# Release points of bulk loads and casts in a hybrid attention and SSM block on eight cores

## The chip, the cores and the metric

The kernel runs on the 8 cores of one Trainium2 chip. Every core takes one of the 8 sequences and the whole set of weights, and the cores don't speak to each other. The metric is the device time of the slowest core. Each core has a matrix engine (TensorE: PE for its matmuls, PEld for its weight loads), a vector engine (VectorE, DVE), a scalar engine (ScalarE, ACT), GpSimd (POOL) and a queue engine (SyncE, SP). Transfers are issued on two queues: SP's, which carries plain copies and transposes, and POOL's, which carries the bulk weight loads that cast float32 to bf16 on the way.

## The reference, cut to what matters

One decoder block over 2048 tokens of width 2048. One input projection gives q, k, v and the SSM's input u; attention over a window of 128 and an S5 state-space model (SSM) run side by side; their normed outputs go through one output projection and a SwiGLU.

```
proj = rms_norm(x) @ w_in                     # 2560 columns: q 1024, k 256, v 256, u 1024
attn = sliding_window_attention(rotary(q), rotary(k), v, sinks)
z    = gelu(s5_ssm(u))                        # 64 groups of 16 channels, 64 complex states each
ssm  = z * sigmoid(z @ w_glu + b_glu)
h    = x + rms_norm(concat[rms_norm(attn), rms_norm(ssm)] @ w_o)
out  = h + rms_norm((silu(n @ w_gate) * (n @ w_up)) @ w_down),  n = rms_norm(h)
```

## The kernel before, in words

**How the order comes about.** The program is first recorded as a list of operations with their dependencies. A planner (`Prog.schedule`) then walks through it with cost formulas for each engine and both DMA queues, and always gives an engine the ready operation with the smallest `prio`. What comes out is one fixed order for each engine. On the chip every engine works through its order strictly; an operation that waits holds up all behind it on the same engine. All recorded operations carry the line of the planner's emit loop (L433), so that they are told apart by their tiles.

**The stages.** x is normed and transposed into `xnT`. `proj_u(0)` and `proj_u(1)` make u in 32 steps of 16 matmuls each (`usteps[0]` to `usteps[31]` are the ScalarE copies that end them); their weights lie in `ws[0]` and `ws[1]` (ws.6 and ws.7 in the profile). The SSM works on 32 pairs of groups (`ssm_pair(q)`), in eight batches of four pairs. Each batch b needs tables from `prep(b)`: `A1s[b % 2]` (A1.44, A1.45) is computed on VectorE and transposed by DMA into `A1Ts[b % 3]` (A1T.67 to A1T.69); `Kst` is copied by eight small DMAs into `KTs[b % 3]` (KT.73 to KT.75). `prep(b)` for b of 3 to 7 stands behind pairs 3, 7, 11, 15 and 19. A new `A1s` tile may be written only when the transpose that reads its old content has landed. The pairs have the smaller `prio` (10 to 41), the projections the larger one, so that the steps of `proj_u(1)` (100), v (200), k (210) and q (220 and more) fill the matrix engine where the SSM leaves it free.

**The loads around the change.** `load_h` loads one piece of 256 columns of `w_in` (1 MB in bf16) into one of the three buffers `wh` (wh.8 to wh.10): v, k, and then q in four pieces. wh.8 and wh.9 lie over `ws[0]`, wh.10 over the second half of `ws[1]`. The loads of v and k wait for the SSM's second u tile (`ur`, 1). A piece of q consists of two stretches of 128 columns that lie 256 columns apart, and is loaded by two DMAs. `cast_wo` casts one of 16 rows of `w_o` into a scratch tensor: nine wait for steps of u, seven for pairs of the SSM; four casts of `w_glu` (`glscr`) also wait for pairs. Their readers come much later, with the GLU and the output projection.

**The end of the output projection.** `oproj(tt)` normalizes a tile of 128 tokens, and a DMA transpose brings `hn` (hn.145, one buffer) into `hnT`. Then `gate_up(0)` starts: `unit(0, u)` loads a raw piece of `w_gate` or `w_up` of 1 MB (`raw`), VectorE makes five combinations of it (`wsm`), and 7 products of 8 matmuls follow, two of them straight from `raw`. Unit 2 of the first block has a buffer of its own, `raw2` (raw.153), over the sixth output weight tile, and its load waits for the transpose of tile 14. The accumulators of unit 2 begin with the two `ev` buffers that lie over `hn`.

Of the kernel before, what the change touches and what calls it, by code (L numbers as in the profile page):

```python
# [481 lines left out]
def build_nc():  # L482
    nc = bass.Bass("TRN2", target_bir_lowering=False, dynamic_dma_scratch_size=8192)

    def din(name, shape, dt=F32):
        return nc.dram_tensor(name, list(shape), dt, kind="ExternalInput").ap()
# [10 lines left out]
    w_in = din("w_in", [D, 2560])  # L497
# [15 lines left out]
    def sb(nm, off, shape, dt):  # L513
        cnt[0] += 1
        return nc.alloc_sbuf_tensor_at("%s.%d" % (nm, cnt[0]), list(shape), dt, offset=BASE + off)
# [4 lines left out]
    P = Prog(nc)  # L520
    V, A, G, T = P.V, P.A, P.G, P.T
    with ExitStack() as st:
# [53 lines left out]
        w_in_v = w_in.rearrange("(c p) n -> p c n", p=128)  # L576
# [203 lines left out]
        usteps = []  # L780
# [25 lines left out]
        qr2 = [sb("qr2", RK + 6144 + 1024 * i, [128, 512], BF16) for i in range(2)]  # L806
        nh_ = [0]

        def load_h(segs, rk=()):
            w = wh[(0, 1, 2, 0, 1, 2)[nh_[0]]]  # L810
            nh_[0] += 1
            o_ = 0
            for c0, n in segs:
                P.dma(w[:, :, o_:o_ + n], w_in_v[:, :, c0:c0 + n], q="gpsimd", rk=rk)
                o_ += n
            return w

# [228 lines left out]
        hn = sb("hn", CO, [128, 2048], BF16)  # L1046
# [7 lines left out]
        def cast_wo(n, op):  # L1054
            P.dma(woscr[n // 2, :, n % 2, :], w_o_v[:, n, :], q="gpsimd", after=(op,), wk=[("wo", n // 2, n % 2)])
# [59 lines left out]
        def next_ev(blk, lo=0):  # L1115
            n = len(ev[blk]) - lo
            ne[0] += 1
            return ev[blk][lo + ne[0] % n][:, :]
# [27 lines left out]
        def product(lhs, rhs):  # L1146
            bk = pbk[0] % 8
            pbk[0] += 1
            with P.group():
                for c in range(8):  # L1150
                    T.matmul(ps[:, bk, :], lhsT=lhs(c), rhs=rhs[:, c, :], start=(c == 0), stop=(c == 7))
            return ps[:, bk, :]

        def unit(blk, u, w_v, s):
            par = (u + blk) % 2
            r, m = raw[blk][par], wsm[blk][par]
            if blk == 0 and u == 2:
                r = raw2
            P.dma(r[:, :, :], w_v[:, :, s * 256:(s + 1) * 256], q="gpsimd", wk=[("gu", blk, u)],
                  rk=[("hn", 14)] if blk == 0 and u == 2 else (), lat=12.0 if blk == 0 and u < 2 else 0.0)  # L1160
            a11, a21 = r[:, 0:8, 0:128], r[:, 0:8, 128:256]
            a12, a22 = r[:, 8:16, 0:128], r[:, 8:16, 128:256]
            V.tensor_tensor(out=m[:, 0, :, :], in0=a11, in1=a22, op=ALU.add)
            V.tensor_tensor(out=m[:, 1, :, :], in0=a21, in1=a11, op=ALU.subtract)
            V.tensor_tensor(out=m[:, 2, :, :], in0=a21, in1=a22, op=ALU.add)
            V.tensor_tensor(out=m[:, 3, :, :], in0=a11, in1=a12, op=ALU.add)
            V.tensor_tensor(out=m[:, 4, :, :], in0=a12, in1=a22, op=ALU.subtract)
            n1, n2, n3 = xe[blk]
            (b11, b12), (b21, b22) = XB
            acc = {k: [next_ev(blk), False] for k in (21, 12, 11, 22)}  # L1170

            def into(k, prod, sign):
                o_, seen = acc[k]
                if seen:
                    V.tensor_tensor(out=o_, in0=o_, in1=prod, op=ALU.add if sign > 0 else ALU.subtract)
                else:
                    A.activation(out=o_, in_=prod, func=AF.Copy, scale=float(sign))
                    acc[k][1] = True
            how = {1: (lambda c: m[:, 0, c, :], n3, ((11, 1), (22, 1))),
                   2: (lambda c: m[:, 2, c, :], b11, ((21, 1), (22, -1))),  # L1180
                   3: (lambda c: r[:, c, 0:128], b12, ((12, 1), (22, 1))),
                   4: (lambda c: r[:, 8 + c, 128:256], n1, ((21, 1), (11, 1))),
                   5: (lambda c: m[:, 3, c, :], b22, ((12, 1), (11, -1))),
                   6: (lambda c: m[:, 1, c, :], n2, ((22, 1),)),
                   7: (lambda c: m[:, 4, c, :], b21, ((11, 1),))}
            for i in (4, 2, 5, 7, 6, 3, 1) if blk == 0 and u == 0 else (4, 3, 1, 2, 5, 6, 7):
                lhs, rhs, uses = how[i]
                prod = product(lhs, rhs)
                for k, sign in uses:
                    into(k, prod, sign)  # L1190
            return [acc[k][0] for k in (21, 12, 22, 11)]
# [104 lines left out]
        for q in range(32):  # L1296
            P.prio = 10.0 + q
            ssm_pair(q)
            P.prio = 60.0 + q
            last = P.ops[-1]  # L1300
            if q in (8, 10, 12, 14, 16, 18, 20):
                cast_wo(9 + (8, 10, 12, 14, 16, 18, 20).index(q), last)
            if q in (9, 13, 17, 21):
                i = (9, 13, 17, 21).index(q)
                P.dma(glscr[:, i, :], w_glu_v[:, 4 + i, :], q="gpsimd", after=(last,), wk=[("gl", i)])
            if q % 4 == 3 and q < 20:
                P.prio = q - 4.0
                prep(q // 4 + 3)
# [2 lines left out]
        V.memset(v1[:, 1:17, :, 64:65], 1.0)  # L1311
        ur = [("ur", 1)]
        P.prio = 59.0
        wv = load_h(((1280, 256),), ur)
        wk_ = load_h(((1024, 256),), ur)
        P.prio = 200.0
        proj_h("v", wv)
        P.prio = 210.0
        proj_h("k", wk_)
        def load_q(a):  # L1320
            c0 = 512 * (a // 2) + 128 * (a % 2)
            return load_h(((c0, 128), (c0 + 256, 128)))
        P.prio = 59.0
        wq = [load_q(a) for a in (0, 1)]
        for a in range(2):
            P.prio = 220.0 + 10 * a
            proj_h("q", wq[a], 2 * a)
        P.prio = -300.0
        zconv()
        P.prio = 59.0  # L1330
        wq = [load_q(a) for a in (2, 3)]
        for tt in range(NT):
            P.prio = 240.0 + tt
# [45 lines left out]
def _host_layouts(inp):  # L1379
    f32 = np.float32  # L1380
    sm = np.zeros((128, NSM), f32)
    half = 32
    sm[:, C_INVF:C_INVF + 32] = (np.float32(10000.0) ** (-np.arange(half, dtype=f32) / np.float32(half))).astype(f32)[None, :]
    sm[:, C_SINK:C_SINK + 16] = inp["sinks"][0][None, :]
    sm[:, C_KT:C_KT + 17] = np.concatenate([np.arange(7, -1, -1), np.arange(0, 9)]).astype(f32)[None, :]
    sm[:, C_DSK:C_DSK + 64] = np.tile(inp["d_skip"][0].T, (8, 1))
    a_re, a_im, ldt = inp["a_re"][0], inp["a_im"][0], inp["log_dt"][0]
    b2 = np.zeros((128, 2, 32, 16), f32)
    c2 = np.zeros((128, 2, 32, 16), f32)
    for b in range(2):  # L1390
        rows = slice(64 * b, 64 * b + 64)
        sm[rows, C_ARA:C_ARA + 32] = a_re[b::2, :].T
        sm[rows, C_AIA:C_AIA + 32] = a_im[b::2, :].T
        sm[rows, C_LDA:C_LDA + 32] = np.broadcast_to(ldt[b::2][None, :], (64, 32))
        b2[rows, 0] = inp["b_re"][0][b::2].transpose(1, 0, 2)
        b2[rows, 1] = inp["b_im"][0][b::2].transpose(1, 0, 2)
        c2[rows, 0] = inp["c_re"][0][b::2].transpose(2, 0, 1)
        c2[rows, 1] = inp["c_im"][0][b::2].transpose(2, 0, 1)
    gv = np.zeros((5, D), f32)
    gv[0] = inp["g_pre_mix"][0]  # L1400
    gv[1] = inp["g_post_mix"][0]
    gv[2] = inp["g_pre_ffn"][0]
    gv[3] = inp["g_post_ffn"][0]
    gv[4, :1024] = inp["g_attn_out"][0]
    r = np.arange(1024)
    pm = (r // 128) * 128 + 16 * (r % 8) + (r % 128) // 8
    w_in = np.concatenate([inp["w_in"][0][:, :1536], inp["w_in"][0][:, 1536:][:, pm]], axis=1)
    w_glu = inp["w_glu"][0][pm][:, pm]
    w_o = np.concatenate([inp["w_o"][0][:1024], inp["w_o"][0][1024:][pm]], axis=0)
    sm[:, C_GSSM:C_GSSM + 8] = inp["g_ssm_out"][0][pm].reshape(8, 128).T  # L1410
    sm[:, C_BGLU:C_BGLU + 8] = inp["b_glu"][0][pm].reshape(8, 128).T
    return {
        "smalls": sm, "gvecs": gv, "ident": np.eye(128, dtype=f32),
        "ctab": np.broadcast_to(np.arange(256, dtype=f32)[None, :], (128, 256)).copy(),
        "b2": b2.reshape(128, 2, 512), "c2": c2.reshape(128, 2, 512),
        "w_in": np.ascontiguousarray(w_in), "w_glu": np.ascontiguousarray(w_glu),
        "w_o": np.ascontiguousarray(w_o), "w_gate": np.ascontiguousarray(inp["w_gate"][0]),
        "w_up": np.ascontiguousarray(inp["w_up"][0]), "w_down": np.ascontiguousarray(inp["w_down"][0]),
    }
# [14 lines left out]
```

How the kernel before makes its waits and increments, by code:

```python
            def run(eng, e):  # L420
                for op in self.order[e]:
                    w = waits[op.idx]
                    att = None
                    if w and e != "tensor":
                        att = w[0]
                        w = w[1:]
                    for s, v in w:
                        eng.wait_ge(sems[s], v)
                    if op.load is not None:
                        eng.preload_act_table_set(SET_NAME[op.load])
                    inst = None
                    for (m, a, kw) in op.calls:
                        inst = getattr(eng, m)(*a, **kw)
                        if att is not None:
                            inst._wait_ge(sems[att[0]], att[1])
                            att = None
                    if op.dma:
                        inst.then_inc(sems[op.sem], 16)
                    elif op.signal:
                        inst.then_inc(sems[e], 1)
                if e == "sync":
                    for d in self.last_dmas:
                        eng.wait_ge(sems[d.sem], d.val)
```

## Time and profile before

| | us |
|---|---|
| median of 3 runs (2609.4 to 2612.86) | 2612.28 |
| the profiled execution | 2606.16 |
| span of its slowest core (core 5) | 2604.6 |
| PE busy in the span | 2469.4 (95%) |
| DVE busy | 1556.5 (60%) |
| ACT busy | 827.4 (32%) |
| POOL busy | 567.3 (22%) |

A wait is listed with the engine that waits and the operation whose end released it. The granted clock is a share of TensorE's full speed. "To landing" is the time from a DMA's issue to the moment it is complete. The profiled execution's own time is 1.6 us above the span of its slowest core.

### The profile page before, as it was taken

The numbers are of one execution on the slowest core, as the hardware profiler recorded it, in microseconds if no ns is written. First come the engines' busy times: TensorE is split into PE (matmuls) and PEld (weight loads), VectorE is DVE, ScalarE is ACT, GpSimd is POOL, SyncE is SP. The second block draws the span as 40 slices with busy tenths as digits, with TensorE's granted clock in tenths as the row PEclk, the third lists the DMA queues.
The fourth block names the chain that finished last, engine by engine and source line by source line (L and its number), as shares of the span: only waits on it lengthen the run. The fifth ranks groups of instructions, "written<-read, shape, count | busy, mean of one in ns | idle before, by whom it ended". The sixth has DMA issues, their size and how long they took to land.

```text
span 2604.6 us, 33566 instructions; the slowest of 8 cores (2585.3 to 2604.6 us)
## 1 busy us (share of the span) xinstructions
PE 2469.4 (95%) x12896; PEld 1207.0 (46%) x12896; DVE 1556.5 (60%) x2436; ACT 827.4 (32%) x1634; POOL 567.3 (22%) x650
## 2 busy tenths in 40 slices
PE   4999889988999889999999999999999999999998
PEld 2545658843444334444444444444444444444443
DVE  6856674768767688777777300017888887710003
ACT  5534443376555432322222000003222223200002
POOL 0235735754333200100101111100100101111112
PEclk9878879999999999999999999999999999999999
DMA  9688837576778987676666967749999966775557
GB/s 241 167 132 122 116 92 97 86 185 164 195 172 194 195 147 123 83 95 82 88 91 86 189 105 110 109 69 158 181 176 177 139 88 83 95 120 76 75 105 241
DMA packets 463643, 341.80 MB, mean 131 GB/s; under 512 B 180224, under 2 KB 424320, under 8 KB 454528
## 3 DMA queue, kind: packets, MB, share of 16 engines
q0 software_dynamic: 260944, 173.10, 49.5%
q1 hardware_dynamic: 202544, 166.57, 25.6%
q8 instruction: 106, 1.74, 0.3%
q14 instruction: 49, 0.40, 0.1%
HBM read 406.65 MB, written 63.96 MB: 181 GB/s over the span
## 4 chain that ended last, share of the span: by engine, by line
PE 81%; DMA 7%; DVE 7%; ACT 2%; issue 2%; POOL 1%; SPq 0%; POOLq 0%; ACTq 0%; DVEq 0%
PE ps L433 81%; DMA ws.6_48<-w_in 2%; DVE M1.2_44 L433 1%; DMA KT.73_115<-Kst.54_96 1%; DVE ast.26_68 L433 1%; DVE ast.27_69 L433 1%; DMA raw.151_193<-w_up 1%; DMA PT.129_171<-Pb.125_167 1%; DMA A1T.67_109<-A1.45_87 1%; DMA PT.129_171<-Pb.126_168 1%; DVE xr.140_182 L433 1%; DMA hnT.146_188<-hn.145_187 0%; DVE hn.145_187 L433 0%; DMA zraw.111_153<-zscr 0%; DMA A1T.69_111<-A1.45_87 0%
## 5 line engine op out<-in xcount | busy, mean ns | idle before, releaser
L433 ACT ACTIVATE ps<-ps 128x512 f32<-128x512 f32 x96 | 55.8, 581 | 351.6 <-DVE ev.179_221 L433 138.5
L433 DVE TENSOR_TENSOR hf.238_280<-ps,gpo.193_235 128x512 f32<-128x512 f32 x16 | 11.1, 691 | 243.4 <-ACT junk.147_189 L433 233.6
L433 PE MATMUL ps<-hnT.146_188,wsm.154_196 128*128 128x512 bf16 x528 | 121.0, 379 | 1.1 <-DVE wsm.154_196 L433 1.1
L433 PE MATMUL ps<-hnT.146_188,wsm.155_197 128*128 128x512 bf16 x528 | 121.1, 379 | 0.0
L433 PE MATMUL ps<-hnT.146_188,wsm.157_199 128*128 128x512 bf16 x528 | 121.1, 379 | 0.0
L433 PE MATMUL ps<-hnT.146_188,wsm.156_198 128*128 128x512 bf16 x528 | 121.1, 379 | 0.0
L433 DVE TENSOR_TENSOR wsm.157_199<-raw.152_194 128x1024 bf16<-128x1024 bf16 x110 | 68.9, 684 | 85.3 <-DMA raw.152_194<-w_gate 83.2
L433 ACT ACTIVATE junk.147_189<-ps 128x512 bf16<-128x512 f32 x16 | 9.6, 597 | 253.4 <-PE ps L433 253.4
L433 POOL DMA_DIRECT2D raw.152_194<-w_gate x22 | 25.2, 1145 | 257.1 <-PE ps L433 160.1
L433 PEld LDWEIGHTS ps<-hnT.146_188,wsm.154_196 128*128 128x128 bf16 x528 | 51.6, 98 | 63.6 <-issue 1.6
L433 PEld LDWEIGHTS ps<-hnT.146_188,wsm.155_197 128*128 128x128 bf16 x528 | 51.7, 98 | 62.3
L433 PEld LDWEIGHTS ps<-hnT.146_188,wsm.157_199 128*128 128x128 bf16 x528 | 51.7, 98 | 62.3
L433 PEld LDWEIGHTS ps<-hnT.146_188,wsm.156_198 128*128 128x128 bf16 x528 | 51.7, 98 | 62.3
L433 POOL DMA_DIRECT2D raw.151_193<-w_up x22 | 25.1, 1140 | 252.5 <-PE ps L433 136.6
L433 DVE TENSOR_TENSOR wsm.156_198<-raw.151_193 128x1024 bf16<-128x1024 bf16 x110 | 70.1, 683 | 15.9 <-DMA raw.151_193<-w_up 15.9
L433 POOL DMA_DIRECT2D raw.150_192<-w_up x22 | 25.2, 1144 | 248.2 <-DVE wsm.154_196 L433 163.6
L433 PE MATMUL ps<-xnT.1_43,ws.7_49 128*128 128x512 bf16 x256 | 71.5, 446 | 0.0
L433 POOL DMA_DIRECT2D raw.149_191<-w_gate x21 | 24.1, 1149 | 214.1 <-PE ps L433 181.4
L433 DVE TENSOR_TENSOR wsm.154_196<-raw.149_191 128x1024 bf16<-128x1024 bf16 x105 | 65.5, 684 | 8.5 <-DMA raw.149_191<-w_gate 8.5
L433 DVE TENSOR_TENSOR wsm.155_197<-raw.150_192 128x1024 bf16<-128x1024 bf16 x110 | 68.6, 682 | 0.0
L433 PE MATMUL ps<-xnT.1_43,ws.6_48 128*128 128x512 bf16 x256 | 66.2, 424 | 1.1 <-DVE xnT.1_43 L433 1.0
L433 DVE TENSOR_TENSOR Ab.142_184<-ps,gpm.143_185 128x512 f32<-128x512 f32 x64 | 43.5, 686 | 39.0 <-PE ps L433 38.2
(1371 smaller groups left out, 6232.1 us busy)
## 6 DMA issues: line engine op xcount, KB each, us to landing
raw.150_192<-w_up POOLq DMA_DIRECT2D x22, 1024.0 KB, 9.4
raw.152_194<-w_gate POOLq DMA_DIRECT2D x22, 1024.0 KB, 13.2
raw.151_193<-w_up POOLq DMA_DIRECT2D x22, 1024.0 KB, 12.4
raw.149_191<-w_gate POOLq DMA_DIRECT2D x21, 1024.0 KB, 9.3
woscr<-w_o POOLq DMA_DIRECT2D x16, 512.0 KB, 11.6
xr.140_182<-x SPq DMA_DIRECT2D x8, 1024.0 KB, 6.3
xr.141_183<-x SPq DMA_DIRECT2D x8, 1024.0 KB, 7.1
hscr<-xr.140_182 SPq DMA_DIRECT2D x8, 1024.0 KB, 4.7
```

The source lines that it names most:

```text
L433: inst = getattr(eng, m)(*a, **kw)
```

## The change

- v's load now also waits for `usteps[22]`, k's for `usteps[27]` (both in `proj_u(1)`).
- The last three casts of `w_o` move from pairs 16, 18 and 20 to pairs 20, 22 and 24; the last two of `w_glu` from pairs 17 and 21 to 19 and 23.
- The host orders the columns of q so that a piece is one stretch of 256 columns. It is loaded by one DMA where there were two; the data in the buffer are the same.
- The load of `raw2` waits for the transpose of tile 15, the last one, in place of tile 14.

```diff
-        def load_h(segs, rk=()):
+        def load_h(segs, rk=(), after=()):
...
-                P.dma(w[:, :, o_:o_ + n], w_in_v[:, :, c0:c0 + n], q="gpsimd", rk=rk)
+                P.dma(w[:, :, o_:o_ + n], w_in_v[:, :, c0:c0 + n], q="gpsimd", rk=rk, after=after)
...
-                  rk=[("hn", 14)] if blk == 0 and u == 2 else (), lat=12.0 if blk == 0 and u < 2 else 0.0)
+                  rk=[("hn", 15)] if blk == 0 and u == 2 else (), lat=12.0 if blk == 0 and u < 2 else 0.0)
...
-            if q in (8, 10, 12, 14, 16, 18, 20):
-                cast_wo(9 + (8, 10, 12, 14, 16, 18, 20).index(q), last)
-            if q in (9, 13, 17, 21):
-                i = (9, 13, 17, 21).index(q)
+            if q in (8, 10, 12, 14, 20, 22, 24):
+                cast_wo(9 + (8, 10, 12, 14, 20, 22, 24).index(q), last)
+            if q in (9, 13, 19, 23):
+                i = (9, 13, 19, 23).index(q)
...
-        wv = load_h(((1280, 256),), ur)
-        wk_ = load_h(((1024, 256),), ur)
+        wv = load_h(((1280, 256),), ur, (usteps[22],))
+        wk_ = load_h(((1024, 256),), ur, (usteps[27],))
...
-            c0 = 512 * (a // 2) + 128 * (a % 2)
-            return load_h(((c0, 128), (c0 + 256, 128)))
+            return load_h(((256 * a, 256),))
...
+    qc = np.arange(1024).reshape(2, 2, 2, 128).transpose(0, 2, 1, 3).reshape(1024)
```

## Rows read from the trace of the kernel before

**Rows 1.** All cores: span and mean granted clock.
```profile
core 0: 2602.2 us, clock 0.970
...
core 5: 2604.6 us, clock 0.963
```
**Rows 2.** Core 5, chain that ended last: start, duration, what.
```profile
144.04 14.61 DMA A1T.67_109<-A1.45_87
...
302.59 20.91 DMA KT.73_115<-Kst.54_96
...
929.62 12.75 DMA hnT.146_188<-hn.145_187
```
**Rows 3.** Core 5, VectorE in order: start, duration, operation [idle before, releaser].
```profile
158.67 0.69 DVE L433 TENSOR_TENSOR A1.45_87<-TT.50_92,TT.51_93 128x512 bf16<-128x512 f32 x1 [12.17 <-DMA A1T.67_109<-A1.45_87]
...
188.78 1.35 DVE L433 TENSOR_TENSOR A1.44_86<-TT.50_92,TT.51_93 128x512 bf16<-128x512 f32 x1
```
**Rows 4.** Core 5, TensorE in order, SSM: columns as in the group before.
```profile
163.27 0.37 PE L433 MATMUL ps<-pab.100_142,identb.16_58 128*128 128x256 bf16 x1 [3.81 <-DVE Rb.104_146 L433]
...
167.08 6.36 PE L433 MATMUL ps<-xnT.1_43,ws.7_49 128*128 128x512 bf16 x16
...
325.18 0.37 PE L433 MATMUL ps<-uring.91_133,KT.75_117 128*128 128x256 bf16 x1 [2.10 <-ACT Kst.54_96 L433]
```
**Rows 5.** Core 5, slices: busy time by engine, then clock, DMA share, GB/s.
```profile
150.00:160.00 10.00, 9.46 (x40) 3.74 (x38) 1.33 (x3) 1.72 (x4) 1.65 (x3) 0.81 1.31 155
160.00:170.00 10.00, 6.49 (x21) 2.51 (x22) 9.56 (x20) 3.92 (x11) 1.79 (x2) 0.56 1.06 152
```
**Rows 6.** Core 0, TensorE in order.
```profile
160.93 0.37 PE L433 MATMUL ps<-pab.100_142,identb.16_58 128*128 128x256 bf16 x1 [12.41 <-DVE Rb.104_146 L433]
```
**Rows 7.** Core 5, POOL in order, bulk loads alone.
```profile
132.94 1.15 POOL L433 DMA_DIRECT2D wh.8_50<-w_in  x1 [2.49 <-DMA uring.90_132<-uscr]
...
135.19 1.16 POOL L433 DMA_DIRECT2D wh.9_51<-w_in  x1
...
204.84 1.16 POOL L433 DMA_DIRECT2D wh.10_52<-w_in  x1 [3.83 <-PE ps L433]
...
918.66 1.14 POOL L433 DMA_DIRECT2D raw.153_195<-w_gate  x1 [19.00 <-PE ps L433]
```
**Rows 8.** Core 5, SP's queue in order.
```profile
183.35 1.22 SPq L433 DMA_TRANSPOSE A1T.68_110<-A1.44_86  x1
```
**Rows 9.** Core 5, DMA issues of 150 to 200: KB each, us to landing.
```profile
A1T.68_110<-A1.44_86 SPq DMA_TRANSPOSE x1, 2.9
```
**Rows 10.** Core 5, DMA issues of 230 to 260.
```profile
wh.10_52<-w_in POOLq DMA_DIRECT2D x1, 512.0 KB, 8.8
```
**Rows 11.** Core 5, DMA issues of 385 to 400.
```profile
zraw.111_153<-zscr SPq DMA_DIRECT2D x1, 512.0 KB, 11.0
```
**Rows 12.** Core 5, PE waits of 0 to 1100: us in total, times, longest.
```profile
PE ps L433 <- DMA zraw.111_153<-zscr: 4.9, 1, 4.9
```
**Rows 13.** Core 5, DMA issues of 840 to 1000.
```profile
raw.149_191<-w_gate POOLq DMA_DIRECT2D x4, 1024.0 KB, 10.4
...
raw.153_195<-w_gate POOLq DMA_DIRECT2D x1, 1024.0 KB, 12.7
```
**Rows 14.** Core 5, TensorE in order, start of the gate and up products.
```profile
931.62 1.89 PE L433 MATMUL ps<-hnT.146_188,raw.153_195 128*128 128x512 bf16 x8 [3.46 <-DMA raw.153_195<-w_gate]
...
946.85 1.89 PE L433 MATMUL ps<-xe.159_201,wsm.154_196 128*128 128x512 bf16 x8 [1.25 <-DVE ev.179_221 L433]
949.85 5.34 PE L433 MATMUL ps<-hnT.146_188,wsm.154_196 128*128 128x512 bf16 x24 [1.11 <-DVE wsm.154_196 L433]
```
**Rows 15.** Core 5, VectorE there.
```profile
933.09 3.09 DVE L433 TENSOR_TENSOR wsm.155_197<-raw.150_192 128x1024 bf16<-128x1024 bf16 x5
```
**Rows 16.** Core 5, ScalarE there.
```profile
942.39 0.60 ACT L433 ACTIVATE ev.180_222<-ps 128x512 f32<-128x512 f32 x1 [6.69 <-DMA hnT.146_188<-hn.145_187]
```
**Rows 17.** Core 5, tile hnT from 840 to 975: landing of its five transposes.
```profile
DMA to landing us min/median/max: 3.8/5.2/12.8
```

More of the change, by code:

```diff
@@ L1406, in _host_layouts @@
     pm = (r // 128) * 128 + 16 * (r % 8) + (r % 128) // 8
-    w_in = np.concatenate([inp["w_in"][0][:, :1536], inp["w_in"][0][:, 1536:][:, pm]], axis=1)
+    qc = np.arange(1024).reshape(2, 2, 2, 128).transpose(0, 2, 1, 3).reshape(1024)
+    w_in = np.concatenate([inp["w_in"][0][:, :1024][:, qc], inp["w_in"][0][:, 1024:1536], inp["w_in"][0][:, 1536:][:, pm]], axis=1)
     w_glu = inp["w_glu"][0][pm][:, pm]
```

## The prediction

> **What bounds the kernel now.** I read the cores first: core 5 ends last, core 0 is 2.4 us behind it [rows 1]. A saving counts only as far as the core that ends last has it. Then the page: TensorE is busy for 95% of the span, and its idle time lies in the first 950 us, where the SSM and the output projection are; from there on the gate, up and down products run without a gap. So a change pays by the TensorE time that it frees ahead of 950, in idle time or in clock. The chain of waits shows where transfers stand on the path: a transpose of the SSM's tables of 14.61 us, small copies of 20.91 us, and the last transpose of the output projection of 12.75 us [rows 2].
>
> The first of them is the clearest stall. VectorE stands for 12.17 us at a write to A1.45 that needs the transpose issued at 144.04 [rows 3]. In flight are the loads of v and k, issued at 132.94 and 135.19 [rows 7]. A transpose of the same size with no bulk load beside it landed in 2.9 us [rows 8, 9]. VectorE's order holds the SSM's own steps behind that write. TensorE fills the time with two steps of u and then idles 3.81 us [rows 4]; its clock was 0.81 before and falls to a mean of 0.56, between the levels of 1.2 and 2.4 GHz, in the ten microseconds after [rows 5]. Core 0 idles 12.41 us at the same place [rows 6]: it ran the filler at a higher clock and was through with it sooner. The core that ends last is thus the one that this stall costs least.
>
> **The change part by part, on core 5.**
>
> *v's load.* It leaves 133. The step `usteps[22]` is the one that ends at 167.08 + 6.36 = 173.4 [rows 4]; with the ScalarE copy behind it I take 174.4 for the issue. The stall that goes is worth the idle 3.81 us and the slow clock: of 6.49 us busy at 0.56, at 0.81 only 6.49 x 0.56 / 0.81 = 4.49 would have been needed, 2.0 us [rows 4, 5]. Sum -5.8. That is the upper bound of the gain; the lower is nothing, if the casts still in flight hold the transpose long enough. I take all of it, since the two large loads are the bulk of what is in flight. No engine waits longer for v: u's steps run until about 230, and a load of 1 MB has a median of 10.4 us [rows 13].
>
> What is late next: the transpose of A1T.68 at 183.35 [rows 8]. It was alone and landed at 186.3, and VectorE wrote A1.44 without a wait at 188.78 [rows 3]. Now v's load is in flight, from 174.4 to about 185 alone, and to about 190 with the cast that is released by the same step. If the transpose lands at 191, VectorE stalls 2 us, and TensorE's filler of one step covers nearly all. At the worst it takes 14.61 us as A1T.67 did [rows 2], lands at 198, and the 9.2 us stall stands bare: 0 to +9.2, I take +1.
>
> The Trainium skill, page "DMA: Bandwidth & Descriptors", section "Queues, rings and completion order", has each DMA engine alternate between the queues that have work, a packet at a time. By that rule a transpose beside one loaded queue would take about twice its 2.9 us, an estimate of 5.8, and A1.44 would wait 0.4 us. The rows here don't bear that out: 14.61 against 2.9 is five times. I keep +1; by the rule it would be 0.
>
> *k's load and the first piece of q.* The first half of that piece was issued at 204.84, when TensorE had read the last of what lay there [rows 7]; that is the step after which k's load is now released. The piece itself, now one transfer, can start only where its second half did, after the last step of u. So at 205 1 MB takes the place of half a megabyte, 10.4 against 8.8 us [rows 10, 13], beside the transpose whose VectorE wait is the second stall of this stretch. -1 (a little less in flight, should k come later) to +4 (the whole load in its way); I take +1, near the difference of 1.6. Behind the waiting issue on POOL stand the same table steps as before, since POOL waited for the same step.
>
> *Casts.* The five moved casts are read after 500 us; their own delay costs nothing, as 100 us and more of projections lie between. Their issues (about 0.6 us each) go to POOL places where the pairs' own waits are already. What they and the halved second piece of q leave is the stretch around 300, where the copies of KT.73 took 20.91 us [rows 2], ScalarE's next Kst copy waited for them and TensorE for that, 2.10 us [rows 4]. I take -2.1 (bounds 0 and -2.1, plus what the clock adds). The cover at 310 to 345 is thin, but the KT copies issued then are first read some 20 us later.
>
> *q in one stretch.* Its effect is on the last z tile: TensorE waits 4.9 us [rows 12] for a load that took 11.0 us [rows 11] beside two half loads of q. Two halves at 8.8 us make 17.6 us of queue, one whole load 10.4 [rows 10, 13]; 7 us less lies beside the z tile. Bounds 0 and -4.9; I take half, -2.5.
>
> *raw2 held back.* Before, its load was issued at 918.66, and what released it was TensorE's last read of the output weights under it [rows 7], not tile 14. Tile 15's transpose is issued at 929.62 [rows 2]. What that transpose delays now is ScalarE: `ev.180` lies over `hn` and waits 6.69 us [rows 16], and VectorE with it. So unit 2 could not be evacuated early anyhow; but its products could run. TensorE's idle time from there to 955 was 3.46 + 1.25 + 1.11 = 5.8 us [rows 14]. Now: at 931.62 - 3.46 = 928.2 TensorE has nothing until the first combination of unit 1, 933.09 + 0.6 [rows 15], which is 5.5 us. Five products at 5.34 / 3 = 1.78 us [rows 14] from 933.7 end at 942.6. With raw.153 out of the way the transpose takes less than 12.75, but more than the median of 5.2 [rows 17], since the load of unit 4 is still in flight: I take 8, so 937.6. Load issue and landing, 0.3 + 10.4 [rows 13], make 948.3, so 5.7 us idle. Together 11.2 against 5.8: +5.4, and with the clock that falls behind gaps of this length +6. Bounds: with 3.8 us for the transpose the load lands at 944.1, +1.2; with 12.75 and a load of 12.7 [rows 13] it lands at 955.4, 12.8 us idle, +12.5. Unit 3's load can be no cover: it is issued behind or beside this one on the same queue.
>
> *Sum:* -5.8 + 1 + 1 - 2.1 - 2.5 + 6 = -2.4 us on a span of 2604.6. The execution's own time was 2606.16, which becomes 2603.8. The median of the runs is 6.1 us above that execution; the same difference makes 2609.9.
>
> On a core like core 0 the first term is -12.4 and more, so its sum is near -9; but core 5 sets the end. A difference below 0.2%, 5.2 us, can't be told from none here.
>
> **The rivals.**
>
> *The stall is worth its full size.* If in the timed runs a core like core 0 ends last, the first term is -12.41 - 2.0 [rows 5, 6], A1T.68 takes back 3, k's load 1, q gives -2.5, and with a transpose of tile 15 near its median the hold-back costs 1.2: -11.7; core 5 itself would be at -2.4 - 4.8 = -7.2. By a value between the two the time is about 2603. For it: core 0 is only 2.4 us behind [rows 1], and one execution doesn't fix which core ends last. Against: the profile has core 5 last, and by rows 5 its filler runs at 0.81.
>
> *The stall only moves.* v's load makes A1T.68 what A1T.67 was; the 5.8 us come back, +4.8 on my sum: 2614.7. For it: the release lies 9 us ahead of that transpose. Against: one load in place of two.
>
> *The hold-back decides.* Tile 15's transpose doesn't get faster, because the load of unit 4 alone is enough to hold it; raw.153 lands at 955, TensorE idles there once for 5.5 and once for 12.8 us, and runs at the lower clock after the long one as after 3.81 us in rows 5, for 2 us. +12.5 + 2 in place of +6 turns the sum of -2.4 into +6.1: 2618.4, slower. It decides from a landing of raw.153 later than about 954. For it: 12.7 and 12.75 are what the rows of before have. Against: a third of what was in flight is gone.
>
> *Nothing of it reaches the end.* The planner's order shifts with every changed release, and gains and losses of a few microseconds elsewhere cover it: 2612. I count it with the forecast.
>
> **How the numbers follow.** Forecast 0.37 (own range 2606 to 2615), full-sized stall 0.32, moved stall 0.09, hold-back 0.22. Faster: 0.32 and 0.04 of the forecast's lower edge, 0.36. Slower: 0.22 and 0.02 of its upper edge, 0.24. The rest, 0.40, is no change. The range goes from 2598, below the full-sized stall by what a still better tile 15 gives, to 2620, just over the hold-back case.
>
> **What would show each step.** The write to A1.45 without a wait, and A1T.67 landing in under 7 us, show the first term; VectorE's idle time before A1.44 shows whether it moved. PE's wait for `zraw` below 3 us shows q's. The KT copies around 300 below 12 us show the casts'. For the hold-back: the landing of the last `hnT` transpose, the landing of raw.153, and PE's longest idle time between 925 and 960. The prediction is wrong if core 5's idle time there stays below 7 us, if A1T.68 takes over 12 us, or if another core ends last with the whole of the first stall saved.

## The result and the profile after

Nine runs of the changed kernel have a median of 2631.47 us, nine of the kernel before on the same chip 2612.49. In some executions, whatever the kernel, the four cores of one die run some per cent longer at a lower granted clock; the ratios and mean spans of this document leave those out. The ratio is 1.0073, 95% interval 1.0053 to 1.0093: **slower by about 19 us**, where the forecast was 2609.9 and the range ended at 2620. The profiled execution took 2629.61 us. Cores 0 and 5, which stood at 2602.2 and 2604.6 [rows 1]:

```profile
core 0: 2628.0 us, clock 0.963
...
core 5: 2616.4 us, clock 0.965
```

The two stretches that the prediction spoke of are both worse. First the SSM. These are the queues that issue, on core 0, which now ends last (start, duration, operation): SP's, then POOL's bulk transfers.

```profile
138.75 15.12 SPq L433 DMA_TRANSPOSE A1T.67_109<-A1.45_87  x1
...
181.74 1.57 SPq L433 DMA_TRANSPOSE A1T.68_110<-A1.44_86  x1
```
```profile
130.25 0.57 POOL L433 DMA_DIRECT2D woscr<-w_o  x1
...
135.16 0.56 POOL L433 DMA_DIRECT2D woscr<-w_o  x1 [2.56 <-ACT ust.76_118 L433]
...
137.51 0.54 POOL L433 DMA_DIRECT2D woscr<-w_o  x1 [1.79 <-ACT ust.76_118 L433]
...
147.08 0.57 POOL L433 DMA_DIRECT2D woscr<-w_o  x1 [4.12 <-ACT ust.76_118 L433]
...
175.56 1.22 POOL L433 DMA_DIRECT2D wh.8_50<-w_in  x1
```

v's load is away from 133 and comes at 175.56, as the diff says. But the casts of the output weights, released by u's steps, are still there, and A1T.67 has not become faster. The DMA issues of 120 to 260 on core 0 (us to landing), before and after:

```profile
A1T.67_109<-A1.45_87 SPq DMA_TRANSPOSE x1, 18.0
A1T.68_110<-A1.44_86 SPq DMA_TRANSPOSE x1, 2.8
```
```profile
A1T.67_109<-A1.45_87 SPq DMA_TRANSPOSE x1, 20.1
A1T.68_110<-A1.44_86 SPq DMA_TRANSPOSE x1, 9.7
```

Over the eight cores A1T.67 takes 19.7 to 24.7 us, where it took 14.6 to 20.3, and A1T.68 on seven of them 9.0 to 11.0 (5.9 on core 5), where it took 2.8 or little more. The transpose is not alone in being late. `uring.91`, a load of u that SP issues just ahead of A1T.67, took 9.6 to 13.0 us before and takes 18.7 to 20.5 now. Core 0, before and after (DMA issues of 120 to 160):

```profile
uring.91_133<-uscr SPq DMA_DIRECT2D x1, 512.0 KB, 10.0
```
```profile
uring.91_133<-uscr SPq DMA_DIRECT2D x1, 512.0 KB, 19.8
```

VectorE and TensorE of core 0 there, in order (in brackets the idle time before and its releaser):

```profile
158.89 0.69 DVE L433 TENSOR_TENSOR A1.45_87<-TT.50_92,TT.51_93 128x512 bf16<-128x512 f32 x1 [19.56 <-DMA A1T.67_109<-A1.45_87]
...
191.49 1.26 DVE L433 TENSOR_TENSOR A1.44_86<-TT.50_92,TT.51_93 128x512 bf16<-128x512 f32 x1 [4.11 <-DMA A1T.68_110<-A1.44_86]
```
```profile
163.49 0.37 PE L433 MATMUL ps<-pab.100_142,identb.16_58 128*128 128x256 bf16 x1 [13.89 <-DVE Rb.104_146 L433]
...
193.49 0.37 PE L433 MATMUL ps<-pab.100_142,identb.16_58 128*128 128x256 bf16 x1 [4.34 <-DVE Rb.104_146 L433]
```

The 12.41 us of [rows 6] are 13.89, and a second stall has come behind it, at the write that had no wait in [rows 3]. Core 5, on which the prediction was worked out, lost more: its idle 3.81 [rows 4] became 14.27.

```profile
164.38 0.37 PE L433 MATMUL ps<-pab.100_142,identb.16_58 128*128 128x256 bf16 x1 [14.27 <-DVE Rb.104_146 L433]
```

The slices of [rows 5] show it (busy time by engine, then clock, DMA share, GB/s):

```profile
150.00:160.00 10.00, 0.10 (x1) 0.00 (x0) 0.22 (x1) 0.00 (x0) 0.00 (x0) 0.65 1.01 184
160.00:170.00 10.00, 5.38 (x19) 2.19 (x20) 9.56 (x20) 2.81 (x8) 1.79 (x2) 0.50 0.01 2
```

The second holds the finding in one row: the DMA share is 0.01, TensorE runs at the lower of its levels, 1.2 GHz, after a slice without work, and the transfers are through: what was lost here was lost waiting for them.

Then the output projection. TensorE of core 0, in order:

```profile
945.09 2.72 PE L433 MATMUL ps<-xe.160_202,wsm.155_197 128*128 128x512 bf16 x6 [5.76 <-DVE wsm.155_197 L433]
...
964.69 3.27 PE L433 MATMUL ps<-xe.158_200,raw.153_195 128*128 128x512 bf16 x8 [8.18 <-DMA raw.153_195<-w_gate]
```

and the chain that ended last on this core (start, duration, what), in which the transpose and the load now follow one another:

```profile
940.78 12.10 DMA hnT.146_188<-hn.145_187
...
953.61 10.95 DMA raw.153_195<-w_gate
```

All eight cores idle 5.76 us at `wsm.155` and 3.8 to 14.5 at raw.153, where they had one wait of up to 5.5 [rows 14]. TensorE's idle time of 900 to 990 is 10.8 to 21.5 us a core, 15.0 in the mean, and was 6.1.

From the last z matmul and the last of the output projection one reads where the 22 us lie by which the mean span of the profiled cores grew (2596.4 to 2618.1): the last z matmul comes 6.7 us later (408.4 to 415.1), the stretch between the two grew by 3.5, and the stretch from the output projection's end by 11.5 (1686.1 to 1697.6).

### The profile page after: what moved, and what is told of

It reads as the page before. It is cut to its first block, busy times and chain, and to the rows that moved or that the text cites. A ratio compares the mean times of both kernels' runs of the same rounds, so it can differ in the third digit from the quotient of the medians.

```text
span 2628.0 us, 33350 instructions; the slowest of 8 cores (2605.8 to 2628.0 us)
## 1 busy us (share of the span) xinstructions
PE 2446.8 (93%) x12687; PEld 1204.9 (46%) x12896; DVE 1547.8 (59%) x2436; ACT 826.9 (31%) x1634; POOL 568.3 (22%) x646
## 4 chain that ended last, share of the span: by engine, by line
PE 73%; DMA 12%; DVE 8%; issue 3%; ACT 3%; POOL 1%; POOLq 0%; SPq 0%; DVEq 0%
PE ps L433 73%; DMA raw.151_193<-w_up 2%; DMA raw.152_194<-w_gate 2%; DMA ws.6_48<-w_in 2%; DMA hf.238_280<-hscr 1%; DVE ast.26_68 L433 1%; DMA A1T.69_111<-A1.45_87 1%; DMA A1T.67_109<-A1.45_87 1%; DVE ast.27_69 L433 1%; DVE M1.2_44 L433 1%; DMA PT.129_171<-Pb.125_167 1%; DVE xr.140_182 L433 1%; DMA PT.129_171<-Pb.126_168 1%; DMA zraw.111_153<-zscr 0%; DMA hnT.146_188<-hn.145_187 0%
## 5 line engine op out<-in xcount | busy, mean ns | idle before, releaser
L433 DVE TENSOR_TENSOR wsm.156_198<-raw.151_193 128x1024 bf16<-128x1024 bf16 x110 | 70.2, 685 | 16.3 <-DMA raw.151_193<-w_up 16.3
L433 PE MATMUL ps<-wh.9_51,xnT.1_43 128*128 128x256 bf16 x512 | 65.9, 286 | 0.0
L433 PE MATMUL ps<-wh.10_52,xnT.1_43 128*128 128x256 bf16 x512 | 61.3, 277 | 0.0
## 6 DMA issues: line engine op xcount, KB each, us to landing
raw.152_194<-w_gate POOLq DMA_DIRECT2D x22, 1024.0 KB, 11.3
woscr<-w_o POOLq DMA_DIRECT2D x16, 512.0 KB, 10.2
```

Of the source, the lines that this page charges most:

```text
L433: inst = getattr(eng, m)(*a, **kw)
```

## The experiments

Each takes one part of the change, or answers one question. Their profiled spans scatter from core to core, and the slowest of eight decides a run; so beside each ratio (against runs of the kernel before on the same chip) I give a second figure: the mean span of each die's four cores, and of those means the median over all runs. It is 2598 us for the kernel before (2597.8 and 2598.3 in the two longest series) and 2617.2 for the change: +19, as by the ratio. I call it the mean span below, and its differences are taken from 2598. In the two shorter series of the kernel before, on the chips of e1 to e8, it is about 2600, so differences of 2 us are not told from none.

**The hold-back alone (e1, e9).** The kernel before with one word changed; measured twice. The ratio is the second's.

```
-                  rk=[("hn", 14)] if blk == 0 and u == 2 else (), ...
+                  rk=[("hn", 15)] if blk == 0 and u == 2 else (), ...
```

> The kernel before with one edit: raw2's load waits for tile 15's transpose. Theory A (the hold-back is the larger part of the loss): PE idles about 5.8 us at unit 1's combinations and 4 to 9 us at raw.153, where it idled 1 to 5.5 us, the clock falls behind both, and the time is 8 to 13 us above the kernel before (about 2622). Rival B (the loss comes from the SSM's releases, the hold-back is repaid because ScalarE no longer waits at ev.180): within 4 us of the kernel before.

> The kernel before with unit 2's load released by tile 15's transpose in place of tile 14's, and nothing else; its profile alone (an earlier run) has a last Wo product to end of span 10.7 us longer as a mean of the cores. Theory A (the hold-back costs what its idle time costs): 2612 + 10 = 2622, 2620 to 2625. Theory B (the SSM's loss makes the change's loss, the hold-back is nearly covered): within 0.2% of 2612.

Measured: ratio 1.0022 [0.9998, 1.0045]; mean span 2607.6, +9.5. In the profiles of both runs the stretch behind the output projection grew by 10.7 and 10.9 us, while the last z matmul came as before. Core 4 of the second run, TensorE:

```profile
939.19 3.57 PE L433 MATMUL ps<-xe.160_202,wsm.155_197 128*128 128x512 bf16 x8 [5.76 <-DVE wsm.155_197 L433]
958.19 3.54 PE L433 MATMUL ps<-xe.158_200,raw.153_195 128*128 128x512 bf16 x8 [7.60 <-DMA raw.153_195<-w_gate]
```

Idle time at 900 to 990 is 13.6 us a core (from 6.1), and the mean clock of 900 to 1000 fell from 0.98 to 0.94. The price is 9 to 11 us by mean span and trace; by the ratio alone, whose interval reaches from 0 to 11.7 us, it would not be settled.

**The change without the hold-back (e2).** The edit above taken back.

> The changed kernel with raw2's load released by tile 14 again; all else of the change stays. Theory A: 8 to 13 us below the changed kernel, so 5 to 10 us above the kernel before, the rest of the loss lying in the SSM (last z tile 4 to 10 us later than before in the mean of the cores). Rival B: it stays near the changed kernel, 15 us or more above the kernel before.

Measured: 1.0064 [1.0043, 1.0086]; mean span 2613.0, +15. The last z matmul is 8.7 us late. This is the second theory's number: taken out of the whole change, the hold-back gives back 2 us by the ratios and 4 by mean span, although the stretch behind the output projection is 9.0 us shorter than in the changed kernel. So the prices don't simply add, and at least half of the loss is the SSM's.

**The release of v and k alone (e3, e12).** Measured twice; the ratio is the second's.

```
-        wv = load_h(((1280, 256),), ur)
-        wk_ = load_h(((1024, 256),), ur)
+        wv = load_h(((1280, 256),), ur, (usteps[22],))
+        wk_ = load_h(((1024, 256),), ur, (usteps[27],))
```

> The kernel before with one edit: the loads of v and k released by steps 22 and 27 of u. Theory C (A1T.67 was not held up by these loads but by the casts of w_o and what else is in flight, and v's load now holds A1T.68): A1T.67 lands in 14 to 20 us as before, PE idles 12 us or more behind it, a new idle time of 4 to 5 us appears near 194, and the time is 3 to 8 us above the kernel before. Rival D (the prediction's: the loads held it): A1T.67 lands under 8 us and the time is 3 us or more below the kernel before; the slow A1T.67 of the changed kernel then comes from its other edits.

> The kernel before with v's and k's loads released by steps 22 and 27 and nothing else, for a ratio, which the first run of it did not give. Its profile's last z matmul came 7.8 us later as a mean of the cores. Theory A (this is the SSM's part of the change's loss): 2617 to 2622, 1.002 to 1.004 of before; together with the hold-back's 10 the whole of the change's 19. Theory B (lost in the SSM, won back behind it): within 0.2%.

Measured: 1.0065 [1.0028, 1.0102]; mean span 2608.7, +10.5. A1T.67 took 19.0 to 27.0 us in the two profiles. TensorE idled 13.9 to 21.2 there, 17.6 in the mean where the kernel before has 11.8; 4 to 6 near 195 on most cores, where it has nothing; and 7 near 235, where it has 3.8 to 13.8. The loss is larger than even the theory that the casts hold the transpose had it (3 to 8 us, later 5 to 10). This is the very part of which the forecast expected its largest gain.

**The casts away, the loads left (e4), and both away (e5).** The nine casts that u's steps release are issued behind pairs 22 to 30 instead; e5 has the release of v and k as well.

```
-        for n, i in enumerate((14, 16, 18, 20, 22, 24, 26, 28, 30)):
-            cast_wo(n, usteps[i])
...
+            if 21 < q < 31:
+                cast_wo(q - 22, last)
```

> The kernel before with the nine casts of w_o that follow steps of u moved behind pairs 22 to 30 of the SSM; the loads of v and k stay at 133. Theory C (casts): A1T.67 lands in under 9 us although both loads are in flight, VectorE waits under 5 us at A1.45, and A1T.69 lands in under 8 us too. Rival D (loads): A1T.67 still takes 14 us or more. Rival E (its own queue: the KT copies and a u load issued ahead of it on SP): also 14 us or more, and the issue itself takes long. The time: 5 to 15 us below before by theory C if the late casts cost nothing at 340 and later, no change by D and E.

> The kernel before with the nine casts of the u steps issued behind pairs 22 to 30, and v's and k's loads released by steps 22 and 27: neither loads nor casts are in flight when A1T.67 is issued. Theory A (casts and loads each hold a transpose; casts the longer): A1T.67 lands in under 7 us on most cores (release alone gave 19 to 26, late casts alone 10.9 to 13.5), TensorE's idle time at the first stall falls below 4 us; v's load alone now lies beside A1T.68, which lands in 7 to 12 us, with 2 to 6 us of idle TensorE there. Theory B (the transposes are slow by what SP's queue and the copies ahead of them do, not by bulk data): A1T.67 stays at 10 us or more. The late casts still cost at 300 to 400, so the time is 0 to 10 us above the kernel before, 2612 to 2622, by A; 2620 to 2630 by B.

The landing of A1T.67 in the four combinations, over all cores:

| | v, k issued at about 133 | v, k released later |
|---|---|---|
| casts with u's steps | 14.6 to 20.3 (before) | 19.0 to 27.0 (e3, e12) |
| casts behind pairs 22 to 30 | 10.9 to 13.5 (e4) | 4.7 to 5.3 (e5) |

```profile
A1T.67_109<-A1.45_87 SPq DMA_TRANSPOSE x1, 23.0
```
```profile
A1T.67_109<-A1.45_87 SPq DMA_TRANSPOSE x1, 13.5
```
```profile
A1T.67_109<-A1.45_87 SPq DMA_TRANSPOSE x1, 5.1
```

(core 0 of e12, of e4 and of e5, in the views of DMA issues of 120 to 260; the 18.0 of the kernel before stands above). The first row's ranges overlap when all profiles are taken: with both as before (also e1, e7, e9 and e16) 14.6 to 22.0 us, mean 18.7 of 40 transposes; with the release (also the changed kernel and e2) 19.0 to 27.0, mean 23.0 of 32. The table settles what holds the transpose. Each of the two does by itself, and the casts longer; neither theory of e4 (under 9 us, or 14 and more) had that. With the casts there, taking the loads away makes it 4 us slower; with the casts gone, the same edit takes 6 to 8 us off on each core. In e5 the stall is gone: no core's TensorE idles 1.5 us between 140 and 190.

In time neither is shown to pay. e4 has 1.0016 [0.9999, 1.0032]. For e5 there are two runs (2608.8 and 2615.1 us), too few for a ratio; the mean span of their cores, about 2595, lies 4 us under that of the kernel before on the same chip. In e4's stretch of 350 to 400 TensorE is busy for 33.0 us of 50 (40.9 before) at a DMA share of 1.15: the casts had to go somewhere, and there they stood in the way of the last z tiles.

**q's columns alone (e7), the pairs' casts alone (e16).**

```
-            c0 = 512 * (a // 2) + 128 * (a % 2)
-            return load_h(((c0, 128), (c0 + 256, 128)))
+            return load_h(((256 * a, 256),))
```
```
-            if q in (8, 10, 12, 14, 16, 18, 20):
+            if q in (8, 10, 12, 14, 20, 22, 24):
...
-            if q in (9, 13, 17, 21):
+            if q in (9, 13, 19, 23):
```

> The kernel before with q's columns of a piece adjacent (one transfer a piece) and nothing else. The forecast's term was -2.5 us at TensorE's wait for zraw, within 0 and -4.9. Theory A (zraw waits for the transfers of the whole stretch, q is a small part): the wait for zraw changes by less than 1.5 us as a mean of the cores, ratio within 0.2% of 1. Theory B (the two halves were what held it): the wait falls below 2 us, time 2608 to 2610.

> The kernel before with the five late casts of the pairs moved behind their later pairs, and nothing else. The forecast had -2.1 us at the copies of KT.73 near 300, between 0 and -2.1. Theory A (no part of the loss): within 0.2% of before, the KT.73 copies of 290 to 330 below 12 us. Theory B (casts behind pairs 19 to 24 collide with the last z tiles): TensorE's wait for zraw up by 2 us or more, and 2615 to 2620.

Measured: 0.9998 [0.9976, 1.0019] and 0.9982 [0.9942, 1.0022]; mean spans 2601.6 (+3.5) and 2595.7 (-2.5). Neither can be told from none by its ratio.

**The place of the waiting write (e6, e13).** No transfer's release is changed. What changes is the planner's idea of how long A1's transposes take (from the batch of A1T.67 on), and with it the order that it writes for the engines, VectorE and TensorE above all.

```
-            P.dma(A1T[:, :, :], A1[:, :], transpose=True)
+            P.dma(A1T[:, :, :], A1[:, :], transpose=True, lat=16.0 if b > 2 else 0.0)
```

> The kernel before with one planner's figure changed: the transposes of A1 (from the third table block on) are given 16 us of latency, so that the order written for VectorE and TensorE puts their readers later; no transfer is moved. Theory A (the stall's price is the place of the waiting write in VectorE's order, whatever holds the transpose): VectorE's wait at A1.45 falls from 12 to 20 us to under 8, TensorE's idle time at 150 to 165 halves, last z matmul 3 to 8 us earlier than in the kernel before; time 2602 to 2609. Theory B (the SSM is bound by its chain of transposes, the tables come too late in any order): the idle time moves to 170 to 260 and the time stays within 0.2% of before.

> The kernel before with 16 us for the transposes of A1, once more, beside the two runs that add one part of the change each. 2588 to 2595, 0.991 to 0.993 of before, if the first result stands; nearer to 1 if it was the chip's.

Measured: 0.9918 [0.9898, 0.9937] and 0.9942 [0.9898, 0.9987]; medians 2592.8 and 2591.91 us; mean span 2577.9 and 2577.4, -20. The last z matmul comes 21 us earlier, where 3 to 8 had been expected. Core 0 of the second run, its DMA issues of 120 to 260, then VectorE and TensorE:

```profile
A1T.67_109<-A1.45_87 SPq DMA_TRANSPOSE x1, 18.4
...
A1T.68_110<-A1.44_86 SPq DMA_TRANSPOSE x1, 18.1
```
```profile
155.11 0.69 DVE L433 TENSOR_TENSOR A1.45_87<-TT.50_92,TT.51_93 128x512 bf16<-128x512 f32 x1 [0.45 <-DMA A1T.67_109<-A1.45_87]
```
```profile
170.48 0.27 PE L433 MATMUL ps<-pab.100_142,identb.16_58 128*128 128x256 bf16 x1 [3.12 <-DVE Rb.104_146 L433]
```

A1T.67 is as slow as ever and A1T.68 slower than before, and VectorE waits 0.45 us (at most 2.54, on core 6) where the kernel before has 12.17 [rows 3] on core 5 and 18.08 on this core. This version beats both kernels.

**What of the change costs in this order (e8, e10, e11, e14, e15).** To the 16 us is added: q's adjacent columns (e8), the whole change (e10), the late casts and the release (e11), the release alone (e14), the hold-back alone (e15); the edits are those above.

> The figure of 16 us for the transposes of A1 and q's adjacent columns together: the version that could beat both kernels, if the stall at A1T.67 can be planned around. If both act: 2600 to 2607, the sum of the two alone. If the planner's order is no cure: within 0.2% of 2612.

> The changed kernel with 16 us of latency given to the transposes of A1 in the planner, as in the run of the kernel before that took 0.992 of its time. Theory A (in the SSM the change costs only where the waiting write stands in VectorE's order; the hold-back is a separate price): TensorE's idle time at A1T.67 falls below 5 us though the transpose still takes 18 us and more, and the time is that of the kernel before with this figure, 2592, plus 10 to 11 for the hold-back: 2600 to 2607. Theory B (the released loads cost in the SSM in any order, by TensorE's clock or other transfers): 2608 to 2615.

> The kernel before with the 16 us for A1's transposes, the nine casts of the u steps issued behind pairs 22 to 30, and the loads of v and k released by steps 22 and 27: the order that tolerates a slow transpose and the transfers out of its way. If the waits that are left at 170 (3 us) are the transfers' and nothing is lost later: 2585 to 2592. If the late casts cost at 300 to 400 as they did in the order of before: 2593 to 2605, no better than the figure of 16 us alone (2592).

> The same with the loads of v and k released by steps 22 and 27. With the whole change the same order lost 24 us in the runs, of which the hold-back's idle time is 9 to 11. Theory A (the release costs in any order, since the bulk comes where the stores of u and A1's later transposes are): 8 to 14 us above the run with 16 us alone, 2600 to 2606, last z matmul 6 to 9 us later. Theory B (q's transfer and the moved casts are what is left): within 3 us of it.

> The same 16 us with unit 2's load released by tile 15's transpose and nothing else of the change. Theory A (the hold-back is a price by itself, whatever the SSM does): last z matmul as without it, and 7 to 11 us more behind the last Wo product, 2599 to 2604. Theory B (hold-back nearly covered): within 3 us.

| added to the 16 us | ratio to before | mean span | against 2577.5 |
|---|---|---|---|
| q (e8) | 0.9953 [0.9934, 0.9971] | 2583.6 | +6 |
| late casts, release (e11) | 0.9953 [0.9919, 0.9987] | 2588.9 | +11 |
| release (e14) | 0.9982 [0.9967, 0.9996] | 2590.4 | +13 |
| hold-back (e15) | 1.0001 [0.9970, 1.0032] | 2590.1 | +13 |
| whole change (e10) | 1.0011 [0.9993, 1.0028] | 2596.6 | +19 |

The parts don't add up here: q, release and hold-back make 32 us by this table, the whole change 19. I had expected the whole change at 2600 to 2607 here, with the release at nothing once the order tolerates slow transposes; it was 2616.73. The release costs in this order too, at another place. Core 0 of e14, VectorE, then TensorE:

```profile
251.90 0.27 DVE L433 MEMSET kT.4_46<- 128x256 bf16 x1 [17.27 <-DMA uscr<-ust.76_118]
```
```profile
253.44 0.37 PE L433 MATMUL ps<-pab.102_144,identb.16_58 128*128 128x256 bf16 x1 [14.71 <-DVE Rb.104_146 L433]
```

`kT` lies where u's staging buffer `ust` was, and its memset waits for the last store of u to be read out. That store goes through POOL's queue, where k's load, issued at 190.63, now stands ahead of it besides the casts and q's halves that are there in both; issued at 215.59, it landed in 36.2 us. In the run without the release (e13) the same store, issued at 212.42, landed in 11.5. The memset waits for that store on seven of e14's eight cores, for 5.2 to 20.1 us, and on none of e13's. That of the two released loads it is k's that makes the store late is read from the order on the queue, not tested alone. The DMA issues of 195 to 260 of the two, core 0 (without, then with the release):

```profile
uscr<-ust.76_118 POOLq DMA_DIRECT2D x1, 512.0 KB, 11.5
```
```profile
uscr<-ust.76_118 POOLq DMA_DIRECT2D x1, 512.0 KB, 36.2
```

e15 leaves the last z matmul where it was (386.2 against 387.4) and adds 11.5 us behind the output projection: the hold-back has this price there though the SSM is 21 us faster.

## Why the prediction was wrong

**v's load, -5.8: the step that failed.** "I take all of it, since the two large loads are the bulk of what is in flight." In bytes they were (2 MB, with two or three casts of half a megabyte beside them), but the transpose is not held in proportion to bytes. The lower bound, nothing "if the casts still in flight hold the transpose long enough", came near, but no loss was in this term's bounds (-5.8 to 0). With the release alone TensorE's idle time at this stall grew from 11.8 to 17.6 us in the mean of the cores; the three terms of the release, -3.8 together, came out at +10.5. The bounds should have reached to the other side, because the loads also stood in POOL's queue ahead of casts. On core 0 a cast issued there between 118 and 150 took 24.9 us in the median in the kernel before, and 11.9 in the changed kernel. With nothing ahead of them more of the casts ran just while A1T.67 did, and the landings show it. In the kernel before, during A1T.67's 18.0 us on core 0, v's load landed at 153.3 and one cast, issued earlier, at 138.6; the next came at 156.5, when the transpose was through. In the changed kernel four casts landed during its 20.1 us, at 139.3, 148.0, 152.2 and 158.0. That this order is the reason, and not something else of the release, is argued; the table of four combinations shows the interaction, not its mechanism.

The Trainium skill, "DMA: Bandwidth & Descriptors", section "Queues, rings and completion order", has each DMA engine alternate by packets between the queues that have work, from which the prediction took an estimate of twice the lone time. The estimate of 5.8 us for A1T.68 beside v's load is what core 5 shows (5.9); the other seven cores have 9.0 to 11.0. For A1T.67, whose own time with neither loads nor casts is 4.7 to 5.3, twice would be an estimate of 9.4 to 10.6: near the 10.9 to 13.5 with loads alone, and far from the 19.0 to 27.0 with casts alone.

**A1T.68, +1.** It landed in 9.0 to 11.0 us on seven cores, inside the bounds, and TensorE idled 3.7 to 5.1 us there. On core 5, for which the term was worked out, it took 5.9 and VectorE waited 0.31: right for that core, too small for the one that ends last. The rival that the stall only moves named the place; but the old stall stayed as well.

**k's load, +1.** A1T.69 took 10.4 to 20.6 us, about what it did, and TensorE's idle time there is unchanged within its scatter. Not what the loss hangs on in this order; in the order of e14 its cost, by the order on the queue, is the 36.2 us store.

**Casts, -2.1.** The copies of KT.73 near 300 landed in 4.1 to 6.7 us on core 5 and its largest wait for Kst was 0.85 instead of 2.10 [rows 2, 4]. On the other seven cores that wait was 0.85 before the change too, so there was nothing to gain there. Alone, -2.5 by mean span, within the noise. The mechanism was right, for core 5.

**q in one stretch, -2.5.** Core 5 waited 3.8 us for `zraw` instead of 4.9 [rows 12], core 0 4.9: -1 for core 5, and in the mean of the cores 4.4 after 4.3, and 4.7 with q's columns alone (e7), which gained no time. The halves were not what held that tile.

**raw2, +6.** The mechanism was right: 5.5 us idle at unit 1's combinations was worked out, 5.76 stands in the trace of every core. Two sizes were too small. One is the transpose of tile 15. I took 8 us, "with raw.153 out of the way"; it takes 9.2 to 12.4, and 8.8 to 12.2 with the hold-back alone, where before it took 11.3 to 14.1. Unit 4's load, issued on core 0 ahead of it, is still in flight:

```profile
935.73 1.14 POOL L433 DMA_DIRECT2D raw.149_191<-w_gate  x1 [25.16 <-PE ps L433]
```

raw.153 lands that much later. The other is the clock. With the hold-back alone TensorE's idle time grew by about 7 us (5.4 was worked out), but the stretch by 10.7 and 10.9, so 3 to 4 us of it are products that took longer at a mean clock of 0.94 instead of 0.98; the forecast had 0.6 for that. Measured by itself the hold-back costs 9.5, between the 6 and the upper bound of 12.5. The rival "the hold-back decides" was near in the transpose of core 5 (12.75, measured 12.41) and in its 2 us for the clock, not in the second idle time (12.8, measured 6.86 on core 5).

Sum: forecast -5.8 + 1 + 1 - 2.1 - 2.5 + 6 = -2.4. Measured alone: release +10.5, casts -2.5, q +3.5, hold-back +9.5, together +21 against +19; but taken out of the whole change the hold-back gave back only 4. No single one of the small terms is sure to 2 us. One core was too narrow a base, too: core 0 ended last this time, and core 5, whose cover of filler made the stall cheap before, idled as long as the others.

Left open: why casts hold a transpose, and the copies beside it on SP's queue, longer than the loads do, and whether q's columns cost 3 us or nothing.

## What to carry to other kernels

Before a transfer is blamed for a stall, take the candidates away one at a time and together: of two that overlap, taking away the larger made the stall here longer. Where a small transfer is slow whatever one does, move its reader in the waiting engine's order first; one planner's figure gave 20 us here, where moving bulk transfers gave nothing that could be told from none, or lost. And a bulk load that is moved in a shared queue can make a store behind it late: 36.2 us here instead of 11.5.

## What the runs showed of the hardware

The issue of a DMA transpose can occupy SP for much of the time to its landing. SP spent 1.25 us on A1T.67 with neither loads nor casts in flight (e5, all cores 1.25 or 1.26), 1.86 to 7.0 in the kernel before, and 9.2 to 16.3 in the changed one, 15.12 on core 0. Nothing waited behind it there: SP's next transfer was issued at 181.74.

Bulk transfers on POOL's queue delay small copies on SP's as they delay the transpose. The copies of KT.75 that SP issued just ahead of A1T.67, of 4 to 32 KB, landed in 1.8 to 3.8 us with neither loads nor casts (e5), in 3.2 to 10.2 with the loads alone (e4), and in 6.6 to 21.8 with the casts alone (e3, e12).
